# The first four weight quarters made by halves on two engines, and the constants on another queue

## What is computed

```python
for i in range(DEPTH):
    h = rmsnorm(x, attn_norm[i])
    proj = h @ w_in[i]
    mq, mk, mv, rq, rk, rv, rg = jnp.split(proj, split_points, axis=-1)
    moba_out = from_heads(moba_attention(...))
    ret = retention_chunkwise(rq, rk, rv)
    ...
    x = x + mix @ w_out[i]
    ...
```

## Time and profile before

| | us |
|---|---|
| median of 3 runs | 833.41 |
| lowest and highest | 833.18, 834.48 |
| the profiled execution | 832.74 |
| its span, first to last instruction | 831.0 |
| PE busy | 813.9 |
| DVE, ACT, POOL busy | 494.0, 466.6, 476.9 |

### The profile page before, as it was taken

How to read it: one execution, slowest core, us unless ns; L and a number is a source line. 1 busy time by engine, 2 the same in 40 slices (tenths; PEclk the granted TensorE clock), 3 DMA queues, 4 the chain that set the end, 5 groups by cost and what they waited for, 6 DMA issues and landing times.

```text
span 831.0 us, 16324 instructions
## 1 busy us (share of the span) xinstructions
PE 813.9 (98%) x6295; PEld 730.0 (88%) x6295; DVE 494.0 (59%) x991; ACT 466.6 (56%) x731; POOL 476.9 (57%) x372
## 2 busy tenths in 40 slices
PE   8999999999999999999999999999999999999995
PEld 7998889999999988889989999999898888888883
DVE  3743455761321425672696826357388699999983
ACT  5434645654534656873467433334456488778863
POOL 5997486999999889697854433358876000000000
PEclk9999999999999999999999999999999999999998
DMA  8655244555555454445632221223536599999921
GB/s 328 221 203 203 89 139 159 199 203 202 202 191 200 168 199 174 161 168 160 221 138 86 86 101 55 101 104 141 212 111 261 197 373 371 357 384 349 382 101 50
DMA packets 24141, 160.98 MB, mean 194 GB/s; under 512 B 3200, under 2 KB 3728, under 8 KB 5392
## 3 DMA queue, kind: packets, MB, share of 16 engines
q1 hardware_dynamic: 21456, 154.67, 51.2%
q10 hardware_dynamic: 2624, 5.44, 2.0%
HBM read 157.62 MB, written 1.05 MB: 191 GB/s over the span
## 4 chain that ended last, share of the span: by engine, by line
PE 90%; DVE 5%; ACT 3%; DMA 1%; issue 1%; POOL 1%; SPq 0%; ACTq 0%; DVEq 0%
PE bank L1170 75%; PE bank L1729 3%; PE bank L1948 1%; PE bank L2065 1%; DMA raw<-weights_dram 1%; DVE work L2540 1%; PE bank L1272 1%; DVE bank L2600 1%; ACT w_hi L629 1%; POOL w_lo L588 1%; PE bank L1336 1%; PE bank L1322 1%; DVE best L2599 0%; PE bank L1758 0%; PE bank L1817 0%
## 5 line engine op out<-in xcount | busy, mean ns | idle before, releaser
L588 POOL TENSOR_TENSOR w_lo<-raw,w_hi 128x512 fp32r<-128x512 f32 x368 | 476.7, 1332 | 159.5 <-ACT w_hi L629 159.4
L1170 PE MATMUL bank<-h_hi,w_hi 128*128 128x256 f32 x864 | 245.2, 284 | 0.5 <-POOL w_lo L588 0.5
L1170 PE MATMUL bank<-h_hi,w_lo 128*128 128x256 f32 x864 | 240.0, 278 | 0.0
L1170 PE MATMUL bank<-h_lo,w_hi 128*128 128x256 f32 x852 | 236.2, 277 | 0.0
L629 ACT ACTIVATE w_hi<-raw 128x1024 fp32r<-128x1024 f32 x184 | 188.2, 1059 | 78.1 <-PE bank L1170 44.5
L1170 PEld LDWEIGHTS bank<-h_hi,w_hi 128*128 128x128 f32 x864 | 162.5, 188 | 4.8 <-issue 1.4
L1170 PEld LDWEIGHTS bank<-h_hi,w_lo 128*128 128x128 f32 x864 | 162.5, 188 | 0.0
L1170 PEld LDWEIGHTS bank<-h_lo,w_hi 128*128 128x128 f32 x852 | 160.2, 188 | 0.3
L1170 PE MATMUL bank<-w_hi,g 128*128 128x512 f32 x416 | 134.2, 391 | 0.0
L1170 PEld LDWEIGHTS bank<-w_hi,g 128*128 128x128 f32 x416 | 78.1, 188 | 16.4 <-issue 0.4
L1170 PE MATMUL bank<-w_lo,g 128*128 128x512 f32 x208 | 81.0, 389 | 0.0
(11 more groups left out here) (403 smaller groups left out, 1256.7 us busy)
## 6 DMA issues: line engine op xcount, KB each, us to landing
raw<-weights_dram SPq DMA_DIRECT2D x119, 1024.0 KB, 4.8
spare<-weights_dram SPq DMA_DIRECT2D x18, 1024.0 KB, 6.5
tok<-weights_dram SPq DMA_DIRECT2D x9, 1024.0 KB, 6.0
x_sb<-x_dram SPq DMA_DIRECT2D x2, 512.0 KB, 4.4
work<-final_norm_dram ACTq DMA_DIRECT2D x2, 512.0 KB, 5.0
work<-work ACTq DMA_DIRECT2D x8, 128.0 KB, 4.8
work<-constants_dram ACTq DMA_DIRECT2D x1, 640.0 KB, 5.3
con<-constants_dram ACTq DMA_DIRECT2D x1, 520.0 KB, 3.7
```

The costliest lines, as they stand in the source:

```text
L588: ins = nc.gpsimd.tensor_tensor(w_lo[:, part], raw[:, part], w_hi[:, part].bitcast(F32), ALU.subtract)
L1170: ins = mm(dst, a, b, start=start and n == 0, stop=stop and n == 2, skip_group_check=True)
```

## The change

The diff, without lines that only stand around it:

```diff
@@ -539,9 +539,27 @@
                     .then_inc(sem(f"half_loaded{slot}"), 16)
-            for half in range(3):
+            def load_constants():
+                for dst, src in ((con[:, P:CON_KEPT], con_in[:, P:CON_KEPT]), (con1, con_in[:, CON_KEPT:]),
+                                 (small_raw[:, :], smalls), (p_raw, p_in)):
+                    sp.dma_start(dst, src).then_inc(sem("constants_loaded"), 16)
+            for part, name in enumerate(("first_loaded", "half_loaded0")):
+                own = slice(part * QUARTER, (part + 1) * QUARTER)
+                sp.dma_start(raw[:, own], weights[0, :, own]).then_inc(sem(name), 16)
+            for half in range(1, 3):
                 load_half(half, half)
-            with sp.Fori(0, N_HALVES // 3 - 1) as i:
+            sp.wait_ge(sem("first_low_half"), 3)
+            for half in range(3, 6):
+                sp.wait_ge(sem("lo_done"), 2 * half - 4)
+                if half == 4:
+                    sp.wait_ge(sem("first_low_half"), 4)
+                load_half(half, half - 3)
+                if half == 3:
+                    load_constants()
+            with sp.Fori(1, N_HALVES // 3 - 1) as i:
                 for slot in range(3):
@@ -580,17 +598,23 @@
         def _(pool):
+            def lo_half(r, i):
+                part = slice(r % RING * QUARTER + i * (QUARTER // 2), r % RING * QUARTER + (i + 1) * (QUARTER // 2))
+                return nc.gpsimd.tensor_tensor(w_lo[:, part], raw[:, part], w_hi[:, part].bitcast(F32), ALU.subtract)
             def lo(n, r):
-                pool.wait_ge(sem("hi_done"), n + 1)
-                for i in range(2):
-                    part = slice(r % RING * QUARTER + i * (QUARTER // 2), r % RING * QUARTER + (i + 1) * (QUARTER // 2))
-                    ins = nc.gpsimd.tensor_tensor(w_lo[:, part], raw[:, part], w_hi[:, part].bitcast(F32), ALU.subtract)
-                    if isinstance(n, int) and n == 0 and i == 0:
-                        ins.then_inc(sem("first_low_half"), 1)
+                pool.wait_ge(sem("hi_done"), n + 3)
+                lo_half(r, 0)
+                lo_half(r, 1).then_inc(sem("lo_done"), 1)
+            for r, i, his in ((1, 0, 2), (1, 1, 4), (2, 1, 5), (3, 1, 6)):
+                pool.wait_ge(sem("hi_done"), his)
+                ins = lo_half(r, i)
                 ins.then_inc(sem("lo_done"), 1)
-            for r in range(RING):
+            for r in range(4, RING):
                 lo(r, r)
@@ -605,15 +629,6 @@
                 act_e.dma_start(dst, src).then_inc(sem("first_constants"), 16)
-            def load_constants():
-                for dst, src in ((con[:, P:CON_KEPT], con_in[:, P:CON_KEPT]), (con1, con_in[:, CON_KEPT:]),
-                                 (small_raw[:, :], smalls), (p_raw, p_in)):
-                    act_e.dma_start(dst, src).then_inc(sem("constants_loaded"), 16)
-                act_e.dma_start(turns.bitcast(I32), pos_in.partition_broadcast(P)).then_inc(sem("positions_loaded"), 16)
-                for name in ("router_b", "a_log", "dt_bias"):
-                    act_e.dma_start(row[:, ROW[name]], rows[name].partition_broadcast(P))\
-                        .then_inc(sem("constants_loaded"), 16)
             def hi(q, base=0):
@@ -627,6 +642,12 @@
                 nc.scalar.activation(w_hi[:, ring(q)], raw[:, ring(q)], ACT.Copy).then_inc(sem("hi_done"), 1)
+            def hi_half(q, i):
+                act_e.wait_ge(sem("half_loaded0" if q else "first_loaded"), 16)
+                part = slice(q * QUARTER + i * (QUARTER // 2), q * QUARTER + (i + 1) * (QUARTER // 2))
+                nc.scalar.activation(w_hi[:, part], raw[:, part], ACT.Copy).then_inc(sem("hi_done"), 1)
             def slot_hi_quarter(i):
@@ -697,22 +718,30 @@
             prepare_root()
-            act_e.wait_ge(sem("x_loaded"), 16 * NT)
-            second_squares()
             act_e.wait_ge(sem("first_constants"), 32)
             norm_hi(0, "attn_norm", (0, 1))
-            hi(0)
-            norm_hi(0, "attn_norm", range(2, 6))
-            hi(1)
-            norm_hi(0, "attn_norm", (6, 7))
+            hi_half(0, 0)
+            norm_hi(0, "attn_norm", (2, 3))
+            hi_half(1, 0)
+            hi_half(0, 1)
+            hi_half(1, 1)
+            norm_hi(0, "attn_norm", range(4, KD))
             for q in range(2, LEAD):
                 hi(q)
-            load_constants()
+            def load_rows():
+                act_e.dma_start(turns.bitcast(I32), pos_in.partition_broadcast(P)).then_inc(sem("positions_loaded"), 16)
+                for name in ("router_b", "a_log", "dt_bias"):
+                    act_e.dma_start(row[:, ROW[name]], rows[name].partition_broadcast(P))\
+                        .then_inc(sem("constants_loaded"), 16)
+            hi(LEAD)
+            second_squares()
             for q in range(4 * B_WOUT):
...
                 if tick == 4:
-                    act_e.wait_ge(sem("other_sums"), 1)
+                    act_e.wait_ge(sem("other_sums"), 8)
                     nc.scalar.activation(stat[:, 128:136], agg[:, :, 1], ACT.Sqrt, bias=eps[:, 1:2])\
@@ -724,7 +753,10 @@
                         p_turned_copy(n)
-                hi(q + LEAD)
+                if q:
+                    hi(q + LEAD)
+                if q == 1:
+                    load_rows()
             mix_hi(2, 2)
@@ -1001,7 +1033,7 @@
                     prepare_root()
-                    act_e.wait_ge(sem("other_sums"), 2)
+                    act_e.wait_ge(sem("other_sums"), 9)
                     nc.scalar.activation(stat[:, 96:112], bank[6][:, 0:16], ACT.Sqrt).then_inc(sem("other_roots"), 1)
@@ -1191,13 +1223,14 @@
             def feature_quarter(n, q, dst, h=(h_hi, h_lo), norm=None, middle=None, in_two=False):
-                if isinstance(n, int) and n == 0:
-                    pe.wait_ge(sem("first_low_half"), 1)
+                by_halves = isinstance(n, int) and n in (2, 3)
+                if by_halves:
+                    pe.wait_ge(sem("first_low_half"), n + 1)
                 else:
...
                 for k in range(KD):
-                    if isinstance(n, int) and n == 0 and k == KD // 2:
+                    if by_halves and k == KD // 2:
                         await_quarter(n)
@@ -1376,11 +1409,21 @@
             turn_half(0, 1)
-            keep_warm(3, 4, warm)
-            spread_root(0, 2)
             keep_warm(3, 6, warm)
-            feature_project(B_RQ, 0, norm=0)
-            pe.wait_ge(sem("root_row_ready"), 1)
+            def first_quarters_by_halves():
+                for half in range(2):
+                    for f in range(2):
+                        pe.wait_ge(sem("lo_done" if f else "first_low_half"), half + 1)
+                        ins = half_quarter(f, f, bank[0][:, f * S:(f + 1) * S], range(4 * half, 4 * half + 4), 0, f == 0)
+                        if half:
+                            ins.then_inc(sem("quarter_done"), 1)
+            first_quarters_by_halves()
+            for f in range(2):
+                feature_quarter(2 + f, 2 + f, bank[1][:, f * S:(f + 1) * S])
+            spread_root(0, 4)
             feature_project(B_RK, 1)
@@ -2218,16 +2261,28 @@
                     .then_inc(sem("ret_s_ready"), 1)
+            def first_lo_half(q, i, his, ks=()):
+                norm_lo(0, "attn_norm", ks)
+                dve.wait_ge(sem("hi_done"), his)
+                part = slice(q * QUARTER + i * (QUARTER // 2), q * QUARTER + (i + 1) * (QUARTER // 2))
+                V.tensor_tensor(w_lo[:, part], raw[:, part], w_hi[:, part].bitcast(F32), ALU.subtract)\
+                    .then_inc(sem("first_low_half"), 1)
             V.memset(warm.bitcast(F32), 1.0).then_inc(sem("warm_ready"), 1)
...
             V.memset(eps[:, 1:2], GN_EPS).then_inc(sem("constants_made"), 1)
+            dve.wait_ge(sem("first_constants"), 32)
+            first_lo_half(0, 0, 1, (0, 1))
+            first_lo_half(0, 1, 3, (2, 3))
+            norm_lo(0, "attn_norm", range(4, KD))
+            first_lo_half(2, 0, 5)
+            first_lo_half(3, 0, 6)
             dve.wait_ge(sem("x_loaded"), 16 * NT)
-            norm()
+            norm(scratch=bank[5][:, 0:2])
             widen_root()
+            store_root_row(0, 4)
             V.tensor_scalar(stat[:, 24:26], stat[:, 4:6], 0.5, None, ALU.mult).then_inc(sem("roots_halved"), 1)
-            dve.wait_ge(sem("first_constants"), 32)
-            norm_lo(0, "attn_norm")
-            store_root_row(0, 2)
             store_scaled(B_RQ, 0, rq)
@@ -2278,10 +2333,8 @@
                         ins = V.bn_aggr(agg[:, g, :], bn[:, g, :])
-                        if g < 7:
-                            ins.then_inc(sem("bn_aggr"), 1)
-                    ins.then_inc(sem("other_sums"), 1)
-                    dve.wait_ge(sem("other_sums"), 1)
+                        ins.then_inc(sem("other_sums"), 1)
+                    dve.wait_ge(sem("other_sums"), 8)
```

(2 more changed lines are left out.)

## The result

| | before | after |
|---|---|---|
| median of 22 runs each, us | 833.79 | 835.22 |
| lowest and highest | 832.76, 834.52 | 833.25, 838.33 |
| the profiled execution | 832.74 | 836.87 |
| its span | 831.0 | 835.1 |

The ratio of after to before is 1.0023, with a 95% interval of 1.0015 to 1.0031. The changed kernel is slower by 1.4 us, where 1.7 less was forecast. Four of 93 further runs of the kernel before, taken beside the experiments, show a slower state of the chip (847.8 to 849.6) and are left out of every ratio. The profiled execution of after is 1.65 above its own median, so what its trace shows is a case at the bad end of a wide spread, and the experiments have to tell how much of it the median carries.

A forecast was written before the change was run, and what follows sets the result against it. PE, busy 98% of the span, was taken to bound the kernel, so an earlier start ends it earlier. Profiled 832.74 - 1.7 gained at quarter 4 = 831.0, plus 0.67 to the median, gave 831.7; range 831.0 to 833.7.

The forecast's parts named there:

- First matmul at 9.9: Start of quarter 0 on PE: first real matmul on weights at 9.9 us instead of 11.25.
- Quarter 1's second half done at 15.6: PE at the start: quarter 0 ends at 14.3 and quarter 1 at 15.6 us, with a 0.2 stop.
- POOL 0.45 later for each half that meets DVE: Low halves of the first quarters: POOL's 1.30 becomes 1.75 beside DVE, 0.45 lost per half.
- the case in which each waits for the whole instruction of the other: Rival, DVE and POOL: 0.7 per half, 1.2 for the squares, PE waits 0.4, time 832.1; chance 0.04.
- Roots wide at 20.8: DVE before quarter 4: widening copies start at 19.4, take 1.38, ready at 20.8 us with 0.3 to spare.
- the first rival: Roots late: second widening copy also waits for POOL, wide at 22.1, PE waits 0.6 to 1.4, 832.7; chance 0.10.
- Quarter 4 at 21.6: PE after the 0.5 spread of the roots: quarter 4 starts at 21.6 instead of 23.34, 1.7 gained.
- The load of quarters 8 and 9 landing by 27: Weights on SyncE's queue behind four large constants: out at 17, landing by 27, needed at 28 us.
- The last row landing at 26: Last small constant row on ACT's queue: issued at 20.4, expected at 26 us, could land at 29.
- the point of 28.7: Landing time of the constants from which PE's first decay, wanted at 47.5 after 18.8 of DVE work, is late.
- constants late: Rival: constants landing after 28.7 cost one for one, 30.4 takes the whole gain, 33 gives 836; chance 0.09.
- The clock: Rival: PE's clock falls for 7 us in the stretch from 8.4 to 15.6, 3.5 lost, 835.2; chance 0.04.

The follow-up runs named there:

- the halves alone: The changed kernel with all eight constant transfers back on ACT's queue, ahead of the rounding of quarter 4: 833.09 us, ratio 0.9999.
- the wait filled: The changed kernel with eight warm matmuls of 512 columns ahead of PE's first retention output: 835.51 us, ratio 1.0020.
- ahead of the squares' wait: The changed kernel with positions and three small rows issued on ACT's queue before second_squares, not behind quarter 5's rounding: 832.95 us, ratio 0.9991.
- one quarter later: The changed kernel with the positions and the three small rows issued behind the rounding of quarter 6: 834.61 us, ratio 1.0008.
- the queues alone: The kernel before with four large constants on SP behind the fourth load and small ones on ACT behind quarter 5's rounding: 833.53 us, ratio 1.0000.
- the two kernels that issue it at 45 us: The changed kernel with rows on their own semaphore, issued at quarter 12: 833.09 us; the same with the roots' spread behind quarter 4: 832.79 us.
- one call moved plus one spread delayed: The changed kernel with the rows issued before second_squares and the roots' spread moved behind quarter 4: 832.00 us, ratio 0.9983.

## Why the prediction was wrong, step by step

- **First matmul at 9.9: 10.22.** Right within 0.3. The transposes took 2.21, not 1.97, so the warm matmuls began at 8.69 instead of 8.43. DVE's low half was as late: done at 10.17 (9.49 + 0.68), where 9.72 was forecast.
- **Quarter 1's second half done at 15.6: 16.1**; end of quarter 3 at 21.1: 21.8. The 0.3 from the first matmul, and 0.1 for each quarter at the longer distance, which the sum didn't know. PE has none of the stops that were feared.
- **POOL 0.45 later for each half that meets DVE.** Too little. It took 3.00 for its first two and 5.75 for the next three, 1.5 and 1.9 each instead of 1.3, and the squares 2.31. That is the case in which each waits for the whole instruction of the other, which got 0.04 and should have had most of the weight. The Trainium skill (SBUF — State Buffer, section Who interferes with whom) says just this of VectorE instructions with two SBUF inputs and GpSimd: they exclude each other. These rows agree with it, 0.68 alone against 1.37, 1.46 and 2.31 beside POOL, and the 0.45 that I had read from one pair of rows was perhaps a partial overlap, which no run here shows.
- **Roots wide at 20.8: 22.2.** The term taken as 1.38 for the pair of copies was 2.44. It was the first rival (0.10), with its mechanism and its time right, wide at 22.1. PE waited 0.33 and not its 0.6 to 1.4, since PE itself came 0.7 later than forecast.
- **Quarter 4 at 21.6: 22.72.** The missing 1.1 are 0.3 from the first matmul, 0.3 from there to the end of quarter 3 (the longer distance took 0.45, and the stop of 0.2 at quarter 1 didn't come) and 0.5 for the roots, 0.33 of idle time and PE's restart behind it. Without the late rows this is what the forecast would still have missed: with a semaphore of their own the kernel took 833.39, and not 831.7.
- **The load of quarters 8 and 9 landing by 27: 29.6.** The sum had bytes ahead of it in its own queue and nothing of the small transfers on the other queue. Moving them to quarter 12 gave 26.4. What it cost PE is small, 0.4 from quarter 8 to 12, as POOL's margin took most of it.
- **The last row landing at 26: 30.97.** This step failed, and it decided the sign. Its issue was forecast at 20.4 and stood at 20.06. The duration is what was mis-sized: 5.6 was taken against a row of 8.6, for the reason that 1.6 MB were no longer ahead of it in its queue. The runs show that the bytes ahead in its queue don't set what such a transfer costs. With the 1.6 MB ahead the last row took 8.6 in the kernel before and 10.8 with the halves alone. With only its three neighbours ahead it took 10.9 us in the changed kernel, 11.7 with the wait filled, 9.2 ahead of the squares' wait, 8.9 one quarter later, 7.5 with the queues alone, and 6.9 and 6.4 in the two kernels that issue it at 45 us. No run came down to 5.6. What does set it stays open. The 8.6 of the row would have given 29.0, past the point of 28.7.
- **That point** came out right by two errors that cancel. From the landing to the first decay it took 20.2 instead of 18.8, but PE was ready at 49.0 instead of 47.5, having lost its gain, so the wait began with a landing at 28.8. The rival "constants late" described the cost one for one: 2.0 of waiting for 2.2 too late.
- **The clock** fell, but not in the stretch that its rival named; it fell behind the 2.0 us wait, in the profiled execution. The rival had the wrong trigger, since it looked at the start's short stops and not at what another rival would make.

The two failures, of the row's landing and of the roots, have one root. Each was a place where the nearest row gave a price (8.6; a full turn) and an argument made it lower. And the chances took the rivals as apart, though both hang on the same late squares. When DVE makes the squares behind four halves that take turns with POOL, both the roots and ACT's queue behind them are late; for the rows the sum had this lateness, and only the landing was mis-sized.

## What to carry to other kernels

An instruction that waits also holds the transfers that stand behind it on its queue; when a producer is moved, look at what its consumer's queue issues next, and put transfers that need nothing ahead of the wait. Give a small broadcast transfer the full time that a trace shows for it, whatever is ahead of it, and give it a semaphore of its own if its data is needed later than that of its neighbours. A gain at the start is worth what its thinnest margin downstream lets through: 0.6 at quarter 4 was a loss of 3.7 at quarter 13 in the profiled execution, and one call moved plus one spread delayed kept 0.9 to the end.

## What the runs showed of the hardware

- PE's granted clock was 1.00 up to and through a 2.0 us wait, fell to 0.50 at 51.65, 0.4 us after PE had gone on, and stayed there for 3.4 us, which cost 1.65. After a wait of 1.6 it did not fall, nor with 8 warm matmuls in the gap.
- Successive 256-column matmuls at full clock start 0.113 or 0.118 apart (276 or 281 ns long in the records), for whole quarters at a time. A matmul split in two of 128 columns was followed by the shorter distance in all 120 places (13 traces, up to 450 us) where it fell into a stretch at the longer one. What starts such a stretch isn't known from these runs.
- Some 400 packets with 0.02 MB together, from 26 to 29 us, went with 0.38 MB of everything else there and a DMA share of 0.39; from 23 to 29 us the rest moved 1.13 MB beside the small packets and 1.75 MB without them. Without them the weights' load landed 3.2 us earlier, issued 0.7 earlier.
